# A hybrid state-space and attention inference step: ScalarE's function tables loaded by a dummy activation ahead of its waits

## The chip, the cores and the metric

One core of a Trainium2 chip runs the whole program in one launch. The metric is the device time of one execution in microseconds (us), lower is better; a kernel's time is the median of its runs. The profile is of one execution, and its times count from the start of its span.

## The reference

Two trunk layers over 384 tokens (128 prompt tokens, 256 latent ones) of width 1024, all in float32. Each layer is a mixer and then a mixture of experts, each behind an RMS norm with a shift, a scale and a gate from the conditioning.

```
def trunk_layer(x, mod, g_mix, g_ffn, mixer, p, moe_p, pos, ctx):
    sh1, sc1, gt1, sh2, sc2, gt2 = jnp.split(mod, 6, axis=-1)
    h = rms_norm(x, g_mix) * (1 + sc1) + sh1
    out, state = mixer(h, p, pos, ctx)
    x = x + gt1 * out
    h = rms_norm(x, g_ffn) * (1 + sc2) + sh2
    x = x + gt2 * moe_ffn(h, *moe_p)
```

Layer 0's mixer runs 16 state-space heads in both directions (chunks of 128 tokens, with `decay = exp(...)` of running sums, and `y = rms_norm(y * silu(z), g)` at the end) beside 8 latent attention heads (q and k RMS-normed, softmax). Layer 1's mixer is grouped-query attention with 16 query heads. The experts are 16, of which each token uses 2; their gate is `silu`, the router a sigmoid.

ScalarE is asked for four kinds of function here: Exp (decays, softmax, router), Sqrt (every RMS norm), Silu (conditioning, convolution, z, experts) and Ln (softplus). Copy, Identity and Square run whatever table is loaded.

## The kernel before

The program is written by engine: each engine has one list of instructions, and semaphores order them. TensorE (PE) does matmuls and transposes into PSUM; VectorE (DVE) and ScalarE (ACT) empty the PSUM banks. PE's results go round through five banks in a list of `jobs` of fixed order; each job names the engine that empties it. `take(name)` in ScalarE's list waits until PE has filled the job's bank (`job_done`); `emptied_by` or a `sem_inc` on `free_act` gives the bank back. PE's `fill(name)` waits until the bank of five jobs before has been given back.

The weights come through a ring of eight 1.5 MB slots, loaded by SyncE's queue in the order of use.

The stages, in order of time:

- The first six slots of the modulation weights (`ada(0)` to `ada(5)`). For each, PE multiplies a row of 384 (L467), ScalarE copies it out (`copy_row`, L1144), and PE turns it by three small matmuls (`turn_row`, L479). With row 3, ScalarE squares x (L982), and before row 4 it takes the root (`root_of(0, 0)`, through `root` at L969).
- Layer 0's input projection, the convolution and its Silu.
- The state-space scan: four steps in `STEPS`, of which the last three are full (`i` = 1, 2, 3). A full step has eight "segments": PE spreads a sum, DVE adds the mask (L1722), ScalarE takes Exp (L1226), GpSimd adds two of them (L1908), DVE multiplies (L1732), PE multiplies by x (L834). It ends in a **tail**: DVE forms the gated output (L1748 to L1752, `ysq_ready`), ScalarE squares it and sums the squares (L1234), takes the root of the sum (`ynorm_ready`), DVE inverts it and scales the output (L1754, L1755, `ynormed`), PE transposes it (L863, job `yT`), ScalarE copies it out with a gain (L1241). The other 26 modulation rows are spread over the scan and the preparation of attention (the table `LATE`); two of them lie in each tail, one before the square and one behind the root, and one after the tail.
- The preparation of layer 0's attention: seven blocks of queries and keys, each with a root of its sums (`qk_root`), a normalisation on DVE and transposes (L894) that ScalarE copies out (L1272). The last modulation row is copied in the last turn, between root and copies; PE turns it and drains at once (`late_ada("mla", k)`), and goes on to the transposes behind it.
- Layer 0's attention (`attention("mla", ...)`): 24 units. PE computes scores (L518), DVE their maximum (L1454, `max_ready`), ScalarE Exp with its sum (L1027), PE transposes (L525) and multiplies by the values (L549). The scores of the sixth unit need the bank that ScalarE's first Exp empties.
- The output projection with the residual on DVE, then `moe(0)`: squares, root and router, then the experts.
- Between the layers the three token tiles come one after another: PE mixes a tile's expert rows (L747), DVE adds it to x (L1625), ScalarE squares it (L1000), PE sums (L496), ScalarE takes the root (L969), DVE inverts it (L1380) and scales (L1386), ScalarE shifts (L1013). DVE's list has the first tile's inverse (`normaliser_of_tile(0)`) ahead of the third tile's addition, whose two halves each wait for PE's mixing of that tile.
- Layer 1: input projection (L918) tile by tile with roots, transposes (L906) copied out at L1291, attention with 48 units, output projection, `moe(1)`.

No table load stands in the kernel's text. The build puts an `ACT_TABLE_LOAD` in front of an activation whose function isn't in the loaded table, and the load carries the line of that activation. The helper that gives the last wait its name `link` waits for ScalarE's own instruction just before:

```
            def link(ins):
                n_chain[0] += 1
                ins.then_inc(S["chain_act"], 1)
                act.wait_ge(S["chain_act"], n_chain[0])
```

`moe` already has two dummy activations of one column, `A(table, ones[:, 0:1], ACT.Sqrt)` and the same with Exp (L1062, L1066); `table` is a spare column of `misc` that nobody reads.

Of the kernel before, what the change touches and what calls it, by code (L numbers as in the profile page):

```python
# [26 lines left out]
NT = T // P  # L27
# [49 lines left out]
def build(nc, small_d, x_d, w_d, y_d, stf_d, stb_d, ckv_d, kpe_d, gk_d, gv_d):  # L77
    f32 = mybir.dt.float32
    ALU = mybir.AluOpType
    ACT = mybir.ActivationFunctionType  # L80
# [4 lines left out]
    with ctx:  # L85
# [18 lines left out]
        ident, ones = sm("ident"), sm("ones")  # L104
# [138 lines left out]
        N_PREP = NT + 4  # L243
# [699 lines left out]
        def _(act):  # L943
# [20 lines left out]

            A = act.activation

            def root(out, src, n, scale=1.0):

                return A(out, src, ACT.Sqrt, bias=EPS / (scale * scale), scale=1.0 / (n * scale * scale))  # L969
# [89 lines left out]

            def moe(l):  # L1060
                act.wait_ge(S["x_new"], DC * l + 1)
                A(table, ones[:, 0:1], ACT.Sqrt)  # L1062
                squares(l, 1)
                act.wait_ge(S["tokens_summed"], l + 1)
                root(rt3[6], ps[:, 6, 0:NT], D).then_inc(S["tokens_root"], 1)
                A(table, ones[:, 0:1], ACT.Exp)  # L1066
                act.wait_ge(S["logits_ready"], l + 1)
                A(rt48[0], rt48[1], ACT.Exp, scale=-1.0).then_inc(S["rt_exp"], 1)
                act.wait_ge(S["inverse_spread"], l + 1)
                act.copy(rn_ffn, ps[:, 7, 0:T]).then_inc(S["inverse_copied"], 1)  # L1070
                for n in ("gk", "gv") if l else ():
                    act.wait_ge(outs[n], 16)
                for c in range(6):
                    scale_and_shift(l, c)
                turned_tokens(l, 0)
                for c in range(6, DC):
                    scale_and_shift(l, c)
                turned_tokens(l, 1)
                over = some_beyond(act, l)
                n0 = N_BLOCK * l  # L1080

                def turned_rows(i):
                    if i >= N_BLOCK:
                        return
                    act.wait_ge(S["turned0"], n0 + i + 1)
                    act.copy(xgT[:, i % NR, 0:512], ps[:, 3, :]).then_inc(S["xgT_act"], 1)

                def silu(i):
                    act.wait_ge(S["up_done"], n0 + i + 1)
                    A(sil_of[i % NR], ps[:, i % NR, 0:256], ACT.Silu).then_inc(S["sil_ready"], 1)  # L1090

                def turned_act(i):
                    act.wait_ge(S["act_turned"], n0 + i + 1)
                    act.copy(actT_of[i % NR], ps[:, i % NR, 0:256]).then_inc(S["actT_ready"], 1)

                def rows_out(i):
                    act.wait_ge(S["down0"], n0 + i + 1)
                    if n0 + i >= 2:
                        act.wait_ge(y_stored[i % 2], 16 * ((n0 + i) // 2))
                    act.copy(ysb[i % 2][:, 0:512], ps[:, 6, :]).then_inc(S["y_act"], 1)  # L1100

                def store(i):
                    act.wait_ge(S["y_act"], n0 + i + 1)
                    act.wait_ge(S["y_dve"], n0 + i + 1)
                    act.dma_start(block_of(rows_d, i), ysb[i % 2]).then_inc(y_stored[i % 2], 16)

                for r in range(NR):
                    turned_rows(r)
                for g in range(NG):
                    i = NR * g  # L1110
                    silu(i)
                    silu(i + 1)
                    turned_rows(i + 3)
                    silu(i + 2)
                    turned_rows(i + 4)
                    turned_act(i)
                    turned_act(i + 1)
                    turned_rows(i + 5)
                    rows_out(i)
                    turned_act(i + 2)  # L1120
                    store(i)
                    rows_out(i + 1)
                    store(i + 1)
                    rows_out(i + 2)
                    store(i + 2)

                with act.If(over):
                    B = BEYOND[l]
                    with act.Fori(0, NE) as e:
                        for b in range(N_BEYOND):  # L1130
                            act.wait_ge(B["turned"], e * N_BEYOND + (b + 1))
                            act.copy(xgb[1][:, 0:512], ps[:, 3, :]).then_inc(B["xgT"], 1)
                            act.wait_ge(B["up"], e * N_BEYOND + (b + 1))
                            A(sil_of[0], ps[:, 0, 0:256], ACT.Silu).then_inc(B["sil"], 1)
                            act.wait_ge(B["act_turned"], e * N_BEYOND + (b + 1))
                            act.copy(actT_of[0], ps[:, 5, 0:256]).then_inc(B["actT"], 1)
                            act.wait_ge(B["down"], e * N_BEYOND + (b + 1))
                            act.copy(ysb[0][:, 0:512], ps[:, 6, :]).then_inc(B["y"], 1)
# [11 lines left out]
            for n in range(N_FIRST):  # L1150
                if n == N_SQUARE:
                    squares(0, 0)
                if n == N_SQUARE + 1:
                    root_of(0, 0)
                copy_row(n)
# [50 lines left out]
            for i, (t, full) in enumerate(STEPS):  # L1206
                if i:
                    act.wait_ge(S["xtok_used"], i)
                for k in range(2):
                    b = take("xt", i, k)  # L1210
                    emptied_by(act.copy(xtok[:, 512 * k:512 * k + 512], b[:, :]))
                b = take("bt", i)
                emptied_by(act.copy(Btok, b[:, 0:P]))
                act.wait_ge(S["free_act"], emptied[index[("bt", i)]][1])
                act.sem_inc(S["xtok_ready"], 1)
                if i == 0:
                    late_rows("state")
                if full:
                    for g in range(2):
                        b = take("g", i, g)  # L1220
                        emptied_by(act.copy(Gs2[g], b[:, 0:P]))
                    act.wait_ge(S["free_act"], emptied[index[("g", i, 1)]][1])
                    act.sem_inc(S["g_ready"], 1)
                    for u in range(8):
                        act.wait_ge(S["seg_ready"], 8 * nfull + u + 1)
                        A(dec[u % 6], dec[u % 6], ACT.Exp).then_inc(S["dec_ready"], 1)  # L1226
                        if u % 2:
                            late_rows("unit", i, {1: -1, 5: 0, 7: 1}.get(u))
                    late_rows("unit", i, 2)
                    late_rows("unit", i, 3)  # L1230
                    for n in LATE[("tail", i)][:1]:
                        copy_row(n)
                    act.wait_ge(S["ysq_ready"], nfull + 1)
                    link(A(zs3[:, t, :], ytok, ACT.Square, accum_out=ssd_r))  # L1234
                    root(ssd_r, ssd_r, D).then_inc(S["ynorm_ready"], 1)
                    for n in LATE[("tail", i)][1:]:
                        copy_row(n)
                    for k in range(2):
                        b = take("yT", i, k)
                        for c in range(4):  # L1240
                            ins = A(oTy3[:, 4 * k + c, TILE[t]], b[:, P * c:P * c + P], ACT.Copy, scale=ssdn[:, 4 * k + c:4 * k + c + 1])  # L1241
                        emptied_by(ins)
                    late_rows("end", i)
                    nfull += 1

            by_head = lambda ap, n: ap.rearrange("p (h n) -> p h n", h=n)
            for k in range(N_PREP + 1):
                v = k - 1
                if k:
                    qk_root(v, mss[v % 2], QM, QM ** -0.5 if v < NT else 1.0)  # L1250
                if k < N_PREP:
                    s, x, sq = k - NT, mkt[k % 2], msq[k % 2]
                    for hh in range(2):
# [21 lines left out]
            attention("mla", HM, m_att, mP)  # L1275
            moe(0)

            squares_of(0)
            squares_of(1)
            root_of_tile(0)  # L1280
# [14 lines left out]
            for i in range(NT + 1):  # L1295
                if i < NT:
# [9 lines left out]
                    A(gsq[t], qkv3[:, t, 0:HQ * HD], ACT.Square).then_inc(S["gsq_ready"], 1)  # L1306
                    qk_root(N_PREP + 2 * i, gss[t], HD, HD ** -0.5)
                    qk_root(N_PREP + 2 * i + 1, gss[NT + t], HD, 1.0)
                if i == 0:
                    shift_of_tile(2)  # L1310
                    turn_gqa(gkT3[:, :, P * KSLOT[3]:P * KSLOT[3] + P], "gkT", 3)
                else:
                    t = ORDER[i - 1]
                    for k in range(2):
                        turn_gqa(gqT3[:, 4 * k:4 * k + 4, TILE[t]], "gqT", t, k)
                    turn_gqa(gkT3[:, :, P * KSLOT[t]:P * KSLOT[t] + P], "gkT", t)
# [705 lines left out]
```

## Time and profile before

| | |
|---|---|
| runs | 1074.12, 1074.91 and 1068.78 us; median 1074.12 |
| the profiled execution | 1069.52 us, span 1068.0 us |
| TensorE (PE) busy | 911.9 us, 85% of the span |
| VectorE (DVE) busy | 338.7 us, 32% |
| ScalarE (ACT) busy | 274.6 us, 26%, 660 instructions |
| mean granted TensorE clock | 0.92 of full speed |
| bytes moved by DMA | 259.00 MB, mean 243 GB/s |

Busy times don't add up to the span, since the engines run beside each other. Outside the span the profiled execution has 1.52 us. "Idle" in square brackets is the time for which an engine stood still just before an instruction, with the engine and line that ended it.

### The profile page before, as it was taken

How to read it: one execution, taken by the hardware profiler on the slowest of the kernel's cores; microseconds unless marked ns; L12 is line 12 of the kernel's file. 1: busy time of each engine (PE TensorE's matmuls, PEld its weight loads, DVE VectorE, ACT ScalarE, POOL GpSimd, SP SyncE). 2: the span in 40 equal slices, each digit the busy share in tenths (PEclk: the TensorE clock that was granted, in tenths of full speed). 3: DMA queues.
4: the chain of work that ended last, by engine and by line, in shares of the span. 5: the costliest groups of instructions: out<-in, count | busy, mean ns of one | idle time of the engine just before them, and what ended most of it. 6: DMA issues, size and time to landing. Idle time of an engine off the chain costs nothing.

```text
span 1068.0 us, 14085 instructions
## 1 busy us (share of the span) xinstructions
PE 911.9 (85%) x5747; PEld 495.2 (46%) x5747; DVE 338.7 (32%) x825; ACT 274.6 (26%) x660; POOL 85.1 (8%) x96
## 2 busy tenths in 40 slices
PE   4999988686888889957989986997999957989984
PEld 1555645464644555533332326654655533333324
DVE  0422005645538630040110113374562140110112
ACT  2411023232336520051210112223552041210210
POOL 2400000110100001050000002000000150000002
PEclk8999998977879999967999997999899967999997
DMA  9999999953367302135899977115000335899925
GB/s 383 427 425 386 369 371 412 384 179 118 128 253 288 123 2 108 70 138 217 355 425 423 423 325 289 66 44 203 1 1 2 118 146 209 352 427 404 422 102 186
DMA packets 36339, 259.00 MB, mean 243 GB/s; under 512 B 3408, under 2 KB 3552, under 8 KB 21424
## 3 DMA queue, kind: packets, MB, share of 16 engines
q1 hardware_dynamic: 20448, 198.27, 46.2%
q0 software_dynamic: 12224, 47.01, 11.9%
q10 hardware_dynamic: 3600, 12.78, 3.0%
q8 instruction: 48, 0.79, 0.3%
q14 instruction: 19, 0.16, 0.0%
HBM read 236.73 MB, written 54.87 MB: 273 GB/s over the span
## 4 chain that ended last, share of the span: by engine, by line
PE 72%; DVE 9%; DMA 8%; ACT 6%; issue 3%; POOL 1%; SPq 0%; PEld 0%; DVEq 0%; POOLq 0%; PEldq 0%; ACTq 0%
PE ps L504 21%; PE ps L671 14%; PE ps L693 8%; PE ps L918 6%; DMA U<-expert_rows 3%; PE ps L518 3%; PE ps L655 3%; PE ps L467 2%; DMA ring<-w_in 2%; PE ps L525 2%; PE ps L747 2%; PE ps L549 1%; ACT hT L1052 1%; DMA expert_rows<-U 1%; PE ps L479 1%
## 5 line engine op out<-in xcount | busy, mean ns | idle before, releaser
L671 PE MATMUL ps<-ring,U 128*32 128x512 f32 x1200 | 166.4, 593 | 0.0
L504 PE MATMUL ps<-U,ring 128*128 128x384 f32 x320 | 106.4, 489 | 3.8 <-DVE U L1470 2.5
L671 PEld LDWEIGHTS ps<-ring,U 128*32 128x32 f32 x1200 | 47.2, 110 | 86.0 <-issue 86.0
L693 PE MATMUL ps<-ring,U 128*32 128x512 f32 x672 | 85.7, 594 | 0.0
L504 PEld LDWEIGHTS ps<-U,ring 128*128 128x128 f32 x320 | 59.6, 189 | 48.0 <-issue 5.0
L671 PE MATMUL ps<-hT,U 128*32 128x512 f32 x168 | 73.1, 592 | 0.0
L671 PE MATMUL ps<-U 128*32 128x512 f32 x168 | 73.1, 592 | 0.0
L467 PE MATMUL ps<-ring,cond_w 128*32 128x384 f32 x512 | 58.6, 583 | 15.4 <-ACT cond_w L974 8.5
L655 PE MATMUL ps<-small,U 128*128 128x128 f32 x192 | 32.6, 326 | 39.3 <-DMA U<-expert_rows 37.3
L918 PE MATMUL ps<-ring,hT 128*128 128x384 f32 x192 | 63.2, 488 | 1.5 <-issue 0.8
L504 PE MATMUL ps<-hT,ring 128*128 128x384 f32 x192 | 63.3, 488 | 0.9 <-issue 0.8
L1579 DVE TENSOR_TENSOR U<-ps,U 128x256 f32<-128x256 f32 x24 | 10.1, 422 | 135.2 <-ACT U L1090 135.2
L504 PEld LDWEIGHTS ps<-hT,ring 128*128 128x128 f32 x192 | 36.1, 190 | 27.5 <-issue 3.3
L918 PEld LDWEIGHTS ps<-ring,hT 128*128 128x128 f32 x192 | 36.0, 190 | 27.3 <-issue 3.4
L655 PEld LDWEIGHTS ps<-small,U 128*128 128x128 f32 x192 | 25.4, 165 | 49.7 <-DMA U<-expert_rows 44.6
L518 PE MATMUL ps<-U,hT 64*128 64x128 f32 (+3 forms) x144 | 42.6, 472 | 5.7 <-ACT U L1027 4.0
L747 PE MATMUL ps<-U 128*128 128x128 f32 x192 | 26.4, 307 | 23.4 <-DMA U<-expert_rows,U 23.4
L1587 DVE COPY U<-ps 128x512 f32<-128x512 f32 x24 | 16.6, 692 | 91.3 <-PE ps L693 56.4
L1090 ACT ACTIVATE U<-ps 128x256 f32<-128x256 f32 x24 | 9.2, 385 | 132.0 <-PE ps L671 132.0
L1413 DVE SCALAR_TENSOR_TENSOR xT<-ps,misc,xT 128x128 f32<-128x128 f32 (+1 forms) x32 | 11.9, 412 | 97.6 <-PE ps L504 97.6
L504 PE MATMUL ps<-ring,hT 128*128 128x384 f32 (+1 forms) x144 | 42.0, 451 | 0.5 <-issue 0.5
L1027 ACT ACTIVATE U<-ps,U 128x384 f32<-128x384 f32 (+1 forms) x72 | 36.3, 510 | 21.3 <-PE ps L525 12.8
(298 smaller groups left out, 1285.0 us busy)
## 6 DMA issues: line engine op xcount, KB each, us to landing
ring<-w_in SPq DMA_DIRECT2D x102, 1536.0 KB, 11.1
expert_rows<-w_in POOLq DMA_DIRECT2D x16, 2048.0 KB, 89.5
U<-expert_rows SPq DMA_DIRECT2D x24, 512.0 KB, 6.4
expert_rows<-U ACTq DMA_DIRECT2D x24, 512.0 KB, 9.2
hT<-w_in SPq DMA_DIRECT2D x6, 1536.0 KB, 12.8
U<-w_in SPq DMA_DIRECT2D x6, 1536.0 KB, 16.1
small<-small_in SPq DMA_DIRECT2D x1, 3147.5 KB, 37.3
xT<-x_in SPq DMA_DIRECT2D x1, 1536.0 KB, 16.7
```

The costliest lines, as they stand in the source:

```text
L467: ins = mm(ps[q:q + 32, bank_row, 0:384], cond3[:, k, :], w[:, k, :], start=(k < 4), stop=(k >= 4))
L504: ins = mm(out, lhs(k), rhs(k), start=(k == 0), stop=(k == n - 1))
L518: filled(mm(b[:, 0:nk], q_of(t, h), k_of(h, k0, nk), start=True, stop=True))
L525: ins = pe.transpose(b[:, P * k:P * k + P], Pb[v % N_P][:, P * k:P * k + P], ident)
L655: ins = pe.transpose(ps[:, 3 + h, P * c:P * c + P], xgb[i % NR][:, 512 * h + P * c:512 * h + P * c + P], ident)
L671: ins = mm(ps[q:q + 32, r, :], xgT[:, r, P * k + q:P * k + q + 32], w[e][:, c:c + 512], start=(k == 0), stop=(k == DC - 1))
L693: ins = mm(ps[q:q + 32, 6 + h, :], actT_of[i % NR][:, P * j + q:P * j + q + 32], w[e][:, c:c + 512], start=(j == 0), stop=(j == 1))
L747: ins = mm(ps[:, MIX_BANK[t] + h, P * c:P * c + P], picked[t][q][:, 512 * h + P * c:512 * h + P * c + P], gate_diag[q][t], start=(q == 0), ...
L918: ins = mm(b[:, 0:384], hT[:, k, TILE[t]], w[:, k, :], start=(k == 0), stop=(k == DC - 1))
L1027: A(Pb[u % N_P][:, 0:nk], b[:, 0:nk], ACT.Exp, bias=nm[:, u:u + 1], accum_out=rs[:, u:u + 1]).then_inc(S["e_ready"], 1)
L1413: ins = stt(xT[:, c, SEG[s]], b[:, SEG[s]], gt[:, 2 * c + s:2 * c + s + 1], xT[:, c, SEG[s]], MUL, ADD)
L1587: dve.tensor_copy(ysb[i % 2][:, 512:1024], ps[:, 7, :]).then_inc(S["y_dve"], 1)
```

## The change

A helper `load_table(function)` issues the dummy activation. It replaces the two dummies in `moe` with the same thing, and is called at these new places:

1. at the start, with Sqrt, behind the squares and ahead of `copy_row(3)` and the first root;
2. in each of the three tails, with Sqrt, behind the tail's first modulation row and ahead of the wait for `ysq_ready`;
3. in the first two tails, with Exp, behind the root and ahead of the tail's second modulation row;
4. in the last turn of the preparation of layer 0's attention, with Exp, behind the last root and ahead of the last modulation row and two copies;
5. between the layers, with Sqrt, ahead of the squares of the first tile;
6. in layer 1's projection, with Exp, behind the last two roots.

```diff
+            def load_table(function):
+
+                A(table, ones[:, 0:1], function)
...
             for n in range(N_FIRST):
                 if n == N_SQUARE:
                     squares(0, 0)
+                    load_table(ACT.Sqrt)
                 if n == N_SQUARE + 1:
                     root_of(0, 0)
                 copy_row(n)
...
                     for n in LATE[("tail", i)][:1]:
                         copy_row(n)
+                    load_table(ACT.Sqrt)
                     act.wait_ge(S["ysq_ready"], nfull + 1)
                     link(A(zs3[:, t, :], ytok, ACT.Square, accum_out=ssd_r))
                     root(ssd_r, ssd_r, D).then_inc(S["ynorm_ready"], 1)
+                    if i + 1 < len(STEPS):
+                        load_table(ACT.Exp)
                     for n in LATE[("tail", i)][1:]:
                         copy_row(n)
...
                 if k:
                     qk_root(v, mss[v % 2], QM, QM ** -0.5 if v < NT else 1.0)
+                if k == N_PREP:
+                    load_table(ACT.Exp)
                 if k < N_PREP:
...
             attention("mla", HM, m_att, mP)
             moe(0)
 
+            load_table(ACT.Sqrt)
             squares_of(0)
             squares_of(1)
             root_of_tile(0)
...
                     qk_root(N_PREP + 2 * i, gss[t], HD, HD ** -0.5)
                     qk_root(N_PREP + 2 * i + 1, gss[NT + t], HD, 1.0)
+                    if i == NT - 1:
+                        load_table(ACT.Exp)
```

## Rows read from the trace of the kernel before

**Rows 1.** The page's chain of work that ended last, by engine.

```profile
PE 72%; DVE 9%; DMA 8%; ACT 6%; issue 3%; POOL 1%; SPq 0%; PEld 0%; DVEq 0%; POOLq 0%; PEldq 0%; ACTq 0%
```

**Rows 2.** Timeline of ScalarE: start, duration, instruction, idle before it; start, `moe(0)`.

```profile
26.26 1.28 ACT L969 ACT_TABLE_LOAD   x1
28.09 0.49 ACT L969 ACTIVATE U<-ps 128x384 f32<-128x384 f32 x1 [0.55 <-PE ps L490]
...
397.97 0.20 ACT L1062 ACTIVATE misc<-small 128x1 f32<-128x1 f32 x1 [12.21 <-DVE xT L1413]
```

**Rows 3.** Timeline of all engines, first tail and the segments behind it.

```profile
211.45 1.06 ACT L1234 ACTIVATE U<-U 128x1024 f32<-128x1024 f32 x1 [5.34 <-DVE U L1752]
...
212.61 1.28 ACT L969 ACT_TABLE_LOAD   x1
...
214.01 0.46 ACT L1144 COPY U<-ps 128x384 f32<-128x384 f32 x1
...
215.15 1.97 PE L863 MATMUL ps<-small,U 128*128 128x128 f32 x8 [6.67 <-DVE U L1755]
...
230.32 2.40 DVE L1722 SCALAR_TENSOR_TENSOR hT<-ps,U,small 128x128 f32<-128x128 f32 x8 [0.37 <-PE ps L827]
...
231.60 0.63 ACT L1226 ACTIVATE hT<-hT 128x512 f32<-128x512 f32 x1
```

**Rows 4.** Timeline, second tail: PE ahead of and behind its wait.

```profile
254.90 1.50 PE L467 MATMUL ps<-ring,cond_w 128*32 128x384 f32 x16
...
261.03 1.41 PE L863 MATMUL ps<-small,U 128*128 128x128 f32 x8 [4.63 <-DVE U L1755]
...
263.44 2.79 PE L467 MATMUL ps<-ring,cond_w 128*32 128x384 f32 x16
```

**Rows 5.** Windows: us, busy time of each engine, PE's granted clock, DMA.

```profile
215.00:223.00 8.00, 7.17 (x36) 4.90 (x36) 1.32 (x2) 2.65 (x9) 0.00 (x0) 0.50 0.52 183
...
261.00:270.00 9.00, 8.97 (x53) 6.38 (x54) 0.00 (x0) 4.86 (x15) 0.00 (x0) 0.62 0.63 241
```

**Rows 6.** Timeline, third tail.

```profile
291.98 1.06 ACT L1234 ACTIVATE U<-U 128x1024 f32<-128x1024 f32 x1
...
294.88 0.76 DVE L1755 TENSOR_SCALAR U<-U,misc 128x1024 f32<-128x1024 f32 x1
...
296.29 1.97 PE L863 MATMUL ps<-small,U 128*128 128x128 f32 x8
```

**Rows 7.** Timeline, end of the preparation and start of layer 0's attention.

```profile
350.01 0.21 ACT L969 ACTIVATE U<-U 128x8 f32<-128x8 f32 x1
...
351.16 0.48 ACT L1144 COPY U<-ps 128x384 f32<-128x384 f32 x1 [0.94 <-PE ps L467]
...
352.76 1.05 PE L894 MATMUL ps<-small,U 128*96 128x128 f32 x8 [0.23 <-DVEq L1785]
...
355.76 1.28 ACT L1027 ACT_TABLE_LOAD   x1 [1.08 <-DVE U L1454]
...
357.57 0.91 PE L518 MATMUL ps<-U,hT 96*128 96x384 f32 x2 [0.18 <-ACT U L1027]
```

**Rows 8.** Timeline, last roots of layer 1 and start of its attention.

```profile
737.22 0.20 ACT L969 ACTIVATE U<-U 128x4 f32<-128x4 f32 x1 [0.57 <-DVE U L1433]
...
741.13 0.59 ACT L1291 COPY hT<-ps 128x512 f32<-128x512 f32 x1 [1.83 <-PE ps L906]
...
744.44 1.28 ACT L1027 ACT_TABLE_LOAD   x1 [0.95 <-DVE U L1454]
...
746.24 1.55 PE L518 MATMUL ps<-U,hT 64*128 64x384 f32 x2 [0.92 <-ACT U L1027]
```

**Rows 9.** Timeline between the layers.

```profile
660.68 1.28 ACT L969 ACT_TABLE_LOAD   x1
...
663.27 2.16 DVE L1625 SCALAR_TENSOR_TENSOR xT<-ps,misc,xT 128x128 f32<-128x128 f32 x8
663.49 1.87 PEld L496 LDWEIGHTS ps<-hT,small 128*128 128x128 f32 x16
```

More of the change, by code:

```diff
@@ L1061, in moe @@
                 act.wait_ge(S["x_new"], DC * l + 1)
-                A(table, ones[:, 0:1], ACT.Sqrt)
+                load_table(ACT.Sqrt)
                 squares(l, 1)
@@ L1065, in moe @@
                 root(rt3[6], ps[:, 6, 0:NT], D).then_inc(S["tokens_root"], 1)
-                A(table, ones[:, 0:1], ACT.Exp)
+                load_table(ACT.Exp)
                 act.wait_ge(S["logits_ready"], l + 1)
@@ L1276, in _ @@
             moe(0)
+            load_table(ACT.Sqrt)
             squares_of(0)
@@ L1308, in _ @@
                     qk_root(N_PREP + 2 * i + 1, gss[NT + t], HD, 1.0)
+                    if i == NT - 1:
+                        load_table(ACT.Exp)
                 if i == 0:
```

## The prediction

> **What bounds the kernel now.** I read the page's chain first: TensorE holds 72% of it, ScalarE only 6% [rows 1]. A change on ScalarE can gain only at those few places where TensorE or VectorE stands still for it, and a table load counts there with its own 1.28 us at most. So the question is not how many loads there are but, for each place, who is idle while the load runs, and what comes next if it doesn't. For that I went through the timeline of each place named in the change. The loads are as many after as before: each new dummy takes a load away from the activation behind it. What is added are nine dummies of about 0.20 us each [rows 2].
>
> Two things about the loads are read before any edit is priced. First, a load is already ahead of a wait where the activation has only one: at the start it runs at 26.26 to 27.54, and the root stands 0.55 us more for TensorE; in the expert layer the dummy starts at 397.97 after 12.21 us of idle time, which begins at 385.76 where its load had ended [rows 2]. Second, where the activation waits for two semaphores, as the first Exp of both attentions does, the load itself stands behind one of them (VectorE's maximum, [rows 7, 8]). So part of the change may find nothing left to hide.
>
> A load's price is 1.28 us plus 0.02 us of gaps: in the first tail it begins at 212.61 and the next instruction of ScalarE but one at 214.01, with a root of 0.20 between [rows 3]. The Trainium skill (ScalarE: Activation LUTs, What ACT_TABLE_LOAD costs) gives 1283 ns for the load and some 1380 ns of drain with it, 2.66 us for every switch. The trace agrees on the first number and shows no room for the second. By the page's number each place that gains would gain up to twice as much, 4 us more in all, and the time would be about 1066 us; that is still within one per cent of the median.
>
> **The change part by part.** Negative is faster.
>
> Start (edit 1): nothing. The load is hidden, and TensorE sets the root's start by 0.55 us [rows 2]. At its new place ScalarE stands idle too, before row 3.
>
> First tail (edits 2, 3): this load is on the path. The square starts when VectorE is done, after 5.34 us of idle time; the load, the root, VectorE's inverse and scaling follow one another, and TensorE has been idle for 6.67 us when it starts its transposes at 215.15 [rows 3]. With the load inside the 5.34 us, the root follows the square directly. It must then wait for the square's own result, which the load had hidden. No row shows this wait alone. Below it is nothing; above, the longest gap of a handover in the rows is the 0.23 us of [rows 7]; the square's handover to the load is 0.02. I take 0.05 us, since the wait is on the engine's own result and no drain lies in it, so the gain is 1.30 - 0.05 = 1.25 us, at least 1.05. Behind the root now stand the Exp load and its dummy, 1.28 + 0.20 = 1.48 us, ahead of the modulation row's copy (214.01 before). The root moves from 213.91 to about 212.65, and the copy to 212.65 + 0.10 + 1.48 = 214.2 or 214.3, ended by 214.75. TensorE wants this row when the eight transposes are through, at 215.15 - 1.25 + 1.6 = 215.5 or later, and the first bank of transposes is full at about 215.05. Both come later than the copy, by 0.3 us in the tighter case. The slot of the ring which that copy frees is released 0.2 us later; the next weights are several slots ahead. Cost: nothing.
>
> What the Exp load gives back at its old place, ahead of the next step's first Exp, is nothing either: it ran at 230.30, and that Exp begins at 231.60, while VectorE began the segments at 230.32 with eight in 2.40 us, so the four that this Exp reads were there at 231.52 [rows 3]. The step behind the second tail has the same order of things.
>
> Second tail: the same, -1.25. TensorE is idle 4.63 us before its transposes [rows 4].
>
> Third tail: nothing, perhaps a little tighter. ScalarE doesn't wait before this square (291.98, just behind a copy), so the load is only moved from behind the square to ahead of it, and the dummy is new: the scaling on VectorE would begin at about 294.88 + 0.24 = 295.12 and end at 295.88. TensorE comes out of its modulation row and starts the transposes at 296.29 [rows 6]: 0.4 us of cover is left of 0.65.
>
> Layer 0's attention (edit 4): about nothing, with a gain and a cost of equal size. The gain: the load begins at 355.76 behind the maximum, the first Exp at 357.06 [rows 7]. With the table there, the first Exp starts at 355.78. But TensorE was busy with the first five score blocks until 357.39, and waited only 0.18 us for the sixth. What follows is limited by ScalarE's six Exps in a row; with the load gone they wait for VectorE's maxima instead, and those of a full score block take about as long as the Exps (the sixth is only computed by TensorE from 357.57, 0.18 us earlier at best). Followed block by block, the sixth Exp comes 0.5 us earlier, not 1.3. The cost: the load and dummy now stand at 350.24 to 351.73, and the last modulation row, copied at 351.16 so far, is copied from 351.63: 0.47 later. TensorE waits for it, turns it and drains, and went on to its transposes at 352.76 with 0.23 us of idle time put down to VectorE. If the drain is what took these 0.23 us, the transposes come 0.45 later; if it was VectorE, 0.25. I take 0.45. Net -0.05, between -0.6 and +0.4.
>
> Layer 1's attention (edit 6): -0.9. Load at 744.44, first Exp at 745.73, and here TensorE has been idle for 0.92 us when it gets the bank at 746.24 [rows 8]. That is all it can gain: it finished the five blocks at 745.32. TensorE runs slowly here, 1.55 us for this block and the transposes behind it, so VectorE's maxima are ready before it and all of the 0.92 should come through; the bounds are 0 and 0.92. The load's new place is after the root at 737.22. Three copies stand behind it and move from 737.33 to about 738.85, and end at about 740.8; the next copy waits for TensorE until 741.13, so 0.3 us of cover is left. VectorE needs only the roots, which are ahead of the load.
>
> Between the layers (edit 5): -0.4. The load is on the chain: it starts at 660.68, the root follows, VectorE inverts and adds the third tile from 663.27 [rows 9]. Without it VectorE would be ready 1.28 us sooner, at 661.99. But the second half of that tile is late next: TensorE's mixing goes on until it begins the following sums at 663.5 or 663.6 [rows 9], and VectorE gets it some 0.2 us later, at 663.8. Four of the eight additions are then left, 1.1 us, and the scaling starts at 664.93 instead of 665.35. Gain 0.42; the bounds are 0 and 1.28.
>
> Sum: -1.25 - 1.25 - 0.05 - 0.9 - 0.4 = -3.85 us, or 0.4%. The profiled execution of 1069.52 us (1068.0 of span and 1.52 around it) would become 1065.7 us. That execution was near the fast end of the runs shown, 4.6 us under their median of 1074.12. On the median I predict **1070 us**. Nothing later takes it back: the DMA engines are nearly idle before both output projections, and the weights of the experts wait for slots that TensorE frees, so they move with it.
>
> **The rivals.**
>
> *The clock stays up in the second tail.* Today TensorE's granted clock falls to half after the idle time there: a modulation row takes 1.50 us before it and 2.79 behind [rows 4], and the clock over 261 to 270 is 0.62 [rows 5]. TensorE's idle time falls from 4.63 to 3.4 us. If that keeps it at 2.4 GHz, the row gives 1.29 us and the transposes and small turns around it, which are as much work again, about as much: -2.6 on top, some 1067 us. Against it: in the first tail the idle time stays at 5.4 us, and there the clock is 0.50 behind it [rows 5].
>
> *The clock falls in one place more.* This is the case on the slow side. Every wait of TensorE moves by one or two microseconds against the points at which the clock changes. A further stretch like 215 to 223, where TensorE was busy for 7.17 us at 0.50 [rows 5], does work in it that the full clock does in 3.6, so it costs 3.6 us. It decides from 3.9 us on, so a bit more than one such stretch must be added; with one and a half it is +1.5 us, about 1076 us. The place is the scan, where low and full stretches alternate. For it: nothing holds the clock in place, and the runs shown differ by 6 us with the same program. Against it: the change shortens TensorE's waits there.
>
> *The change doesn't do what it says.* If the load in the tails is not on the path after all, or the root's wait for the square costs as much as the load did, or the cover of 0.3 us in the tails (a copy behind the Exp load) is gone, the two tails give nothing or lose 0.2 each. Then attention and the seam leave -1.3: 1073 us. For it: the loads at the start and in the expert layers are ahead of their waits already [rows 2].
>
> **How the numbers follow.** The forecast as summed has 0.55, the clock that stays up 0.18, the clock that falls once more 0.12, the change without effect 0.12, and 0.03 is left for a load that costs up to twice its row. That last one is the Trainium skill's price for a switch. Around each case lies the spread of the runs, about 3 us to each side. A measurement of this kernel can't tell less than one per cent, 10.7 us. Faster than 1063.4 us is only reached from the fast end of the first rival: 0.07. Slower than 1084.9 would need several low stretches more: 0.03. The range goes from 1067 with 4 off for the spread, 1063, to the slow case at 1076 and half a microsecond more, 1076.5.
>
> **What the profile after would show.** In the first two tails: a load between the copy of row one and the square, root at once behind the square (under 0.15 us), transposes 1.25 us after where they would be, an Exp load behind the root, and no load at the first Exp of the next step, which still starts when VectorE lets it. TensorE's idle time before L863 falls from 6.67 and 4.63 to 5.4 and 3.4. Third tail: transposes directly behind TensorE's own row. Layer 0's attention: TensorE's turn of the last modulation row waits 0.5 us more, the sixth block no longer for ScalarE. Layer 1: the 0.92 us gone. Between the layers VectorE's additions split in two fours with a gap. I would be wrong if ScalarE's root stood long behind the square without a load, if the copies behind the Exp loads became what TensorE waits for, or if the granted clock in 200 to 310 changed by more than these microseconds.

## The result and the profile after

The changed kernel takes 1067.57 us (median of 20 runs), the kernel before 1074.27 (20 runs): ratio 0.9946, 95% interval 0.9930 to 0.9962. That is 5.8 us faster, between 4.1 and 7.5. I had forecast 1070, from a sum of -3.85. One run of a kernel below, others_again, took 1167.52 us at a clock of 0.795: it is in a slower state of the chip, and only the median of its row has it.

The profiled execution is one of the longest of its kernel: 1073.41 us, at a mean granted clock of 0.912, where the 20 runs have 0.918. So its span can't be set against that of before. Its pieces can, each from its own start. From the page: the span, the busy times, the granted clock in 40 slices, and the chain.

```profile
span 1071.8 us, 14094 instructions
...
PE 919.4 (86%) x5747; PEld 500.3 (47%) x5747; DVE 338.5 (32%) x825; ACT 276.7 (26%) x669; POOL 85.0 (8%) x96
...
PEclk8899997688879899977999998998899967999997
...
PE 72%; DVE 8%; DMA 8%; ACT 5%; issue 3%; POOL 1%; PEld 1%; SPq 0%; DVEq 0%; POOLq 0%; PEldq 0%; ACTq 0%
```

Nine instructions more on ScalarE, which are the nine dummies; its share of the chain is 5% for 6. The windows show where this execution lost its time. First before, then after; the columns are those of [rows 5], the clock is the third figure from the end:

```profile
170.00:205.00 35.00, 29.34 (x257) 20.48 (x255) 23.78 (x49) 10.15 (x21) 5.09 (x4) 1.00 1.02 425
```

```profile
170.00:205.00 35.00, 28.18 (x188) 19.89 (x189) 20.87 (x45) 9.03 (x19) 5.08 (x4) 0.79 1.01 405
```

In the same 35 us TensorE ran 257 matmuls before and 188 after. This stretch lies ahead of the first tail, and the two kernels have the same instructions in it, in the same order. At its start the execution after is 0.8 us early; by the first square it is 9.9 us late (221.39 for 211.45); by its last instruction only 3.8. Nor is that the work of the edits: the executions of others_only and others_again, one and the same kernel, have that square at 222.78 and 216.39. So a gain of 3 to 6 us can't be read off one pair of profiles.

The first tail, in order of time:

```profile
220.13 1.23 DVE L1765 TENSOR_TENSOR U<-U 128x1024 f32<-128x1024 f32 x1
221.39 1.06 ACT L1240 ACTIVATE U<-U 128x1024 f32<-128x1024 f32 x1 [2.31 <-DVE U L1765]
222.35 0.19 ACT L1240 ACTIVATION_READ_ACCUMULATOR U<-U 128x1 f32 x1
222.57 0.20 ACT L973 ACTIVATE misc<-misc 128x1 f32<-128x1 f32 x1
222.79 1.28 ACT L969 ACT_TABLE_LOAD   x1
...
223.81 1.28 PE L863 MATMUL ps<-small,U 128*128 128x128 f32 x8 [3.88 <-DVE U L1768]
224.08 0.20 ACT L969 ACTIVATE misc<-small 128x1 f32<-128x1 f32 x1
224.19 0.46 ACT L1148 COPY U<-ps 128x384 f32<-128x384 f32 x1
224.55 2.18 ACT L1249 ACTIVATE U<-ps,small 128x128 f32<-128x128 f32 x8
```

The root stands 0.03 us behind the square's sum (222.54), with no load between, and TensorE's transposes start 2.42 us after the square where it was 3.70 [rows 3]: -1.28. The Exp load runs while VectorE and TensorE go on. The second tail has the same 2.42.

The same timeline at the start of layer 0's attention, at the seam between the layers, and at the start of layer 1's attention; first the rows of before that the last two are measured from:

```profile
659.60 1.06 ACT L1000 ACTIVATE hT<-xT 128x1024 f32<-128x1024 f32 x1 [2.52 <-DVE xT L1625]
...
665.35 2.18 DVE L1386 SCALAR_TENSOR_TENSOR hT<-xT,misc,U 128x128 f32<-128x128 f32 x8
...
743.54 1.78 PE L518 MATMUL ps<-U,hT 64*128 64x128 f32 x10 [0.67 <-ACT U L1291]
...
747.73 0.69 PE L525 MATMUL ps<-small,U 128*128 128x128 f32 x2
```

```profile
353.75 0.21 ACT L973 ACTIVATE U<-U 128x8 f32<-128x8 f32 x1
353.98 1.28 ACT L969 ACT_TABLE_LOAD   x1
...
355.38 0.46 ACT L1148 COPY U<-ps 128x384 f32<-128x384 f32 x1
...
355.90 0.83 PE L479 MATMUL ps<-misc,U 128*128 128x2 f32 x6 [1.15 <-ACT U L1148]
356.96 1.23 PE L894 MATMUL ps<-small,U 128*96 128x128 f32 x8 [0.23 <-issue]
...
664.92 1.06 ACT L1004 ACTIVATE hT<-xT 128x1024 f32<-128x1024 f32 x1 [2.51 <-DVE xT L1638]
...
665.88 0.26 ACT L973 ACTIVATE U<-ps 128x128 f32<-128x128 f32 x1
...
667.40 1.12 DVE L1638 SCALAR_TENSOR_TENSOR xT<-ps,misc,xT 128x128 f32<-128x128 f32 x4 [0.28 <-PE ps L747]
...
669.12 1.13 DVE L1638 SCALAR_TENSOR_TENSOR xT<-ps,misc,xT 128x128 f32<-128x128 f32 x4 [0.59 <-PE ps L747]
670.16 2.18 DVE L1399 SCALAR_TENSOR_TENSOR hT<-xT,misc,U 128x128 f32<-128x128 f32 x8
...
748.37 3.38 PE L518 MATMUL ps<-U,hT 64*128 64x128 f32 x12 [0.68 <-ACT U L1302]
...
749.59 0.37 ACT L1031 ACTIVATE U<-ps,U 128x128 f32<-128x128 f32 x1 [1.27 <-DVE U L1467]
...
751.67 0.72 PE L525 MATMUL ps<-small,U 128*128 128x128 f32 x2
```

Layer 0: from the last root to TensorE's transposes 3.21 us where it was 2.75 [rows 7], +0.46. The 0.23 us ahead of them are still there, now put down to nobody, although VectorE was done earlier against them; what is left in the program at that place is the drain. Layer 1: TensorE's score blocks run on as one group of 12 where the gap of 0.92 us was [rows 8], and from the first scores to the first transposes it is 3.30 us for 4.19, -0.89. These two don't have the same clock: over the first 1.78 us of the scores it was 1.00 in the execution before and 0.50 in that after. At half clock throughout, the three executions without edit 6 (tails_only, mla_only, before_warm) take 4.58 or 4.59 us and seven with it 3.30 to 3.32. So at equal clock the edit takes off 1.28 us, the whole load, and not the 0.92 of the gap. Seam: VectorE's eight additions have become two fours, each waiting for TensorE, as the second half's lateness demanded; from the second tile's square (659.60 before) to the first scaling 5.24 us for 5.75, -0.51.

The start (edit 1) moved nothing that shows: the root waits for TensorE's sum with the load ahead of it or not, and comes at about 28 us where that sum ran at full clock and at 29.4 to 30 where it ran at half clock. Both are seen in kernels with the edit and without it.

The pieces add up to -2 x 1.28 - 0.9 - 0.5 + 0.46 = -3.5 us, or -3.9 with the 1.28 of equal clock in layer 1's attention. The measured gain is 5.8. The experiments ask first whether each piece is what it seems, and then where the other 1.9 to 2.3 us come from.

### The profile page after: what moved, and what is told of

Read it like the earlier page. It is cut to its first block, busy times and chain, and to the rows that moved or that the text cites. A ratio compares the mean times of both kernels' runs of the same rounds, so it can differ in the third digit from the quotient of the medians.

```text
span 1071.8 us, 14094 instructions
## 1 busy us (share of the span) xinstructions
PE 919.4 (86%) x5747; PEld 500.3 (47%) x5747; DVE 338.5 (32%) x825; ACT 276.7 (26%) x669; POOL 85.0 (8%) x96
## 4 chain that ended last, share of the span: by engine, by line
PE 72%; DVE 8%; DMA 8%; ACT 5%; issue 3%; POOL 1%; PEld 1%; SPq 0%; DVEq 0%; POOLq 0%; PEldq 0%; ACTq 0%
PE ps L504 21%; PE ps L671 13%; PE ps L693 8%; PE ps L918 6%; PE ps L518 3%; DMA U<-expert_rows 3%; PE ps L655 3%; PE ps L467 3%; PE ps L747 2%; PE ps L525 2%; DMA ring<-w_in 2%; PE ps L549 1%; ACT hT L1056 1%; DMA expert_rows<-U 1%; PE ps L827 1%
## 5 line engine op out<-in xcount | busy, mean ns | idle before, releaser
L518 PE MATMUL ps<-U,hT 64*128 64x128 f32 (+3 forms) x144 | 46.1, 512 | 4.2 <-ACT U L1031 2.7
```

What stands on the lines that cost most here:

```text
L518: filled(mm(b[:, 0:nk], q_of(t, h), k_of(h, k0, nk), start=True, stop=True))
```

## The experiments

Each kernel was timed in five rounds beside the kernel before. The granted clock has two levels, 1.2 and 2.4 GHz, so 2 x (1 - mean clock) x span is the time that an execution spent at 1.2 GHz. "Low" is its mean over a kernel's runs; its standard error is about 2 us, or 3 with the kernels of six runs (tail_slow, warm_tails, warm_two_tails; the others have 12, after 20). The row of before is from all 87 of its runs in these rounds. That of after is from its own 20, which were timed in other rounds, so its low time is set against before's only across sessions.

| kernel | edits | median us | ratio (95%) | mean clock | low us |
|---|---|---|---|---|---|
| before | | 1073.4 to 1075.3 | 1 | 0.9138 | 184.8 |
| after | 1 to 6 | 1067.57 | 0.9946 (0.9930 to 0.9962) | 0.9179 | 175.2 |
| tails_only | 2, 3 | 1068.91 | 0.9960 (0.9936 to 0.9983) | 0.9153 | 181.0 |
| sqrt_tails | 2 | 1071.12 | 0.9962 (0.9946 to 0.9979) | 0.9135 | 185.0 |
| others_only | 1, 4, 5, 6 | 1074.46 | 0.9997 (0.9975 to 1.0020) | 0.9139 | 184.5 |
| others_again | 1, 4, 5, 6 | 1073.95 | 0.9990 (0.9972 to 1.0008) | 0.9146 | 182.9 |
| mla_only | 4 | 1072.63 | 1.0005 (0.9984 to 1.0027) | 0.9128 | 186.8 |
| layers_att1 | 5, 6 | 1070.26 | 0.9960 (0.9939 to 0.9981) | 0.9186 | 174.0 |
| tails_layers_att1 | 2, 3, 5, 6 | 1066.40 | 0.9937 (0.9916 to 0.9958) | 0.9193 | 172.0 |
| mla_behind_row | 1 to 6, 4 moved | 1067.38 | 0.9942 (0.9919 to 0.9965) | 0.9187 | 173.2 |
| tail_slow | 1 to 6, two switches more | 1081.34 | 1.0088 (1.0053 to 1.0122) | 0.9098 | 194.9 |
| before_warm | none, idle matmuls | 1073.24 | 0.9989 (0.9961 to 1.0016) | 0.9198 | 171.7 |
| warm_tails | as mla_behind_row, idle matmuls | 1067.00 | 0.9912 (0.9886 to 0.9939) | 0.9225 | 165.1 |
| warm_two_tails | the same, fewer | 1063.79 | 0.9924 (0.9899 to 0.9948) | 0.9210 | 167.9 |

### The tails

The kernel is the changed one with the dummies outside the tails taken out.

> Edits 2 and 3 alone (both loads in the tails), the rest as before. My theory (the loads in the first two tails stood on the path): from the square's start to TensorE's transposes 2.42 us where it was 3.70, in both tails; time 2.5 us under before. Rival 'the clock gives the rest': the measured gain of 5.8 us came mostly from the scan's clock, so this kernel alone gains 4 to 5 us. Rival 'no effect': within 0.5 us of before.

Ratio 0.9960, 4.3 us, and 2.42 us in both tails. The spans are as the theory has them, and the time is nearer to the rival's 4 to 5; the interval (1.8 to 6.9 us) holds both.

The third tail is instructive, since the clock decided there. In the executions of before and after, the modulation row ahead of the transposes ran at half clock (2.79 us), and TensorE came last [rows 6]: 4.68 us from the copy to the transposes before, 4.69 after. In this one it ran at full clock, so ScalarE's chain came last:

```profile
296.59 0.48 ACT L1148 COPY U<-ps 128x384 f32<-128x384 f32 x1 [8.13 <-PE ps L467]
297.09 1.28 ACT L969 ACT_TABLE_LOAD   x1
297.95 1.50 PE L467 MATMUL ps<-ring,cond_w 128*32 128x384 f32 x16
298.50 1.04 ACT L1239 ACTIVATE U<-U 128x1024 f32<-128x1024 f32 x1
...
300.91 1.09 PE L863 MATMUL ps<-small,U 128*128 128x128 f32 x8 [1.46 <-DVE U L1762]
```

From the copy to the transposes it is 4.32 us. The kernel without the tails' edits has the same clock there, and 4.08 (from 301.40 to 305.48):

```profile
301.40 0.48 ACT L1148 COPY U<-ps 128x384 f32<-128x384 f32 x1 [8.12 <-PE ps L467]
301.77 1.06 ACT L1239 ACTIVATE U<-U 128x1024 f32<-128x1024 f32 x1
...
302.94 1.28 ACT L973 ACT_TABLE_LOAD   x1
...
305.48 1.09 PE L863 MATMUL ps<-small,U 128*128 128x128 f32 x8 [1.23 <-DVE U L1765]
```

So a load that is moved where ScalarE doesn't wait gains nothing and costs the dummy, 0.24 us, whenever the cover of a slow TensorE is gone.

Edit 2 without edit 3:

```diff
                     root(ssd_r, ssd_r, D).then_inc(S["ynorm_ready"], 1)
-                    if i + 1 < len(STEPS):
-                        load_table(ACT.Exp)
```

> Edit 2 alone: the Sqrt load ahead of the square in the three tails; the Exp load stays at the first Exp of the next step. My theory (the Exp load costs and gives nothing in either place): the same as with edits 2 and 3, 1069.5 us, tails 2.42 us each, and the first Exp of the next step begins 1.3 us after VectorE began the segments, as in before. Rival: the Exp load on the old place now is late, since the tail ends earlier, and costs up to 1.3 us twice.

Ratio 0.9962 beside 0.9960, tails at 2.42. The rival (up to 2.6 us lost) would have given 0.9984, but the difference of the two kernels has an error of 3 us, so the times alone don't exclude it. The rows behind the first tail do:

```profile
234.48 1.28 ACT L1230 ACT_TABLE_LOAD   x1
235.41 1.13 DVE L1727 SCALAR_TENSOR_TENSOR hT<-ps,U,small 128x128 f32<-128x128 f32 x4 [1.28 <-PE ps L827]
236.57 0.63 ACT L1230 ACTIVATE hT<-hT 128x512 f32<-128x512 f32 x1 [0.81 <-DVE hT L1727]
```

The load is over at 235.76, and the Exp stands 0.81 us more for VectorE. It begins 1.16 us after VectorE's segments, and so it does in tails_only, where the load was moved. At its old place this load was hidden, so edit 3 gains nothing.

### A switch more in each tail

```diff
                     link(A(zs3[:, t, :], ytok, ACT.Square, accum_out=ssd_r))
+                    A(misc[:, 244:245], ones[:, 0:1], ACT.Exp)
+                    A(misc[:, 245:246], ones[:, 0:1], ACT.Sqrt)
                     root(ssd_r, ssd_r, D).then_inc(S["ynorm_ready"], 1)
```

> The changed kernel with two more dummies, Exp and Sqrt, between the square and the root of every tail: two more switches there, each 1.28 + 0.20 us by the trace. If a switch costs what its row shows and the tails are on the path, the first two tails take 3.0 us more each and the third 2.6 (0.4 us of cover): 8.6 us over the changed kernel. If a switch costs 2.66 us, as the Trainium skill has it (ScalarE: Activation LUTs, What ACT_TABLE_LOAD costs), it is 14 to 16 us. If the tails are hidden, under 2 us.

1.0088 over 0.9946 is 1.0143, so 15.3 us over the changed kernel, 11 to 19. Going by the time alone, the 2.66 us that the Trainium skill gives for a switch (ScalarE: Activation LUTs, What ACT_TABLE_LOAD costs) look confirmed. The timeline of the first tail says otherwise:

```profile
215.01 0.19 ACT L1240 ACTIVATION_READ_ACCUMULATOR U<-U 128x1 f32 x1
215.21 1.28 ACT L1241 ACT_TABLE_LOAD   x1
216.50 0.20 ACT L1241 ACTIVATE misc<-small 128x1 f32<-128x1 f32 x1
216.71 1.28 ACT L1242 ACT_TABLE_LOAD   x1
218.01 0.20 ACT L1242 ACTIVATE misc<-small 128x1 f32<-128x1 f32 x1
218.12 0.18 ACT L973 ACTIVATE misc<-misc 128x1 f32<-128x1 f32 x1
...
219.34 1.97 PE L863 MATMUL ps<-small,U 128*128 128x128 f32 x8 [8.26 <-DVE U L1770]
```

5.30 us from the square to the transposes for 2.42: two switches with their dummies cost 2.88, and there is no room for a drain of 1.38 us after either. Three tails make 8.6 us, or 8.3 if the third (5.29 us) is set against the 2.79 of the changed kernel's execution, which had some cover. The low time rose with it, from 175.2 to 194.9 us, while TensorE stands 8.26 us ahead of the first tail's transposes.

What a microsecond at low clock is worth can be read off without any edit: over the 87 runs of the kernel before, a line through time against low time has a slope of 0.29 us per us. So 19.7 us more are 5.7, and 8.6 + 5.7 = 14.3 us, beside a difference of means of 13.9. The slope is a correlation in one kernel and not an experiment, and the twelve other kernels, 6 to 20 runs each, have slopes from 0.21 to 0.52; that it fits here is the check that it gets. The low time and the time also come from the same runs, so a fit says that the excess came with the clock and not what moved the clock.

### Does TensorE's idle time bring the clock down?

If so, work without use in the idle time brings it up. Five matmuls go ahead of TensorE's wait, into the bank that the transposes overwrite:

```diff
-                    pe.wait_ge(S["ynormed"], nfull + 1)
+                    yT = [fill("yT", i, 0)]
+                    for _ in range(5):
+                        mm(yT[0][:, 0:T], ident, small[:, OFF["tri_f"][0]:OFF["tri_f"][0] + T], start=True, stop=True)
+                    pe.wait_ge(S["ynormed"], nfull + 1)
...
-                        b = fill("yT", i, k)
+                        b = yT[0] if k == 0 else fill("yT", i, 1)
```

> The kernel before with the same five idle matmuls in each tail and no load moved. Theory A: its low-clock time, 184 us, falls to 170 or less and the time by 3 to 5 us, to about 1069, without any dummy. Theory B: 1073 as before.

> The kernel of the run before with the load behind the row, and in each tail five matmuls of 128x384 by TensorE ahead of its wait for the normalised output, into the bank that the transposes overwrite; they compute nothing that is used (1.6 us at full clock, inside an idle time of 3.7 to 5 us). Theory A (TensorE's idle time in the tails is what brings its clock down, so that a microsecond of idle costs more than itself): the low-clock time per run, twice one minus the mean clock times the span, falls from 173 us to 160 or less, and the time by 3 us or more, to 1064. Theory B (the low stretches come as they come): both unchanged within 2 us.

The clock followed in both: low time 184.8 to 171.7 us with the kernel before, 173.2 to 165.1 on the changed one. For the first, the difference is about six standard errors, and theory B is out; for the second it is two, which alone would show little. The time of the first did not follow as I had said: 0.9989 (1.2 us under before, between 4.2 under and 1.7 over). The second has 0.9912 beside 0.9942, 3.2 us less with an error of 3.8. The matmuls were dearer than reckoned, 0.70 us each for my 0.33 (3.49 us for five at full clock), and stood on the path: 3.98 us from square to transposes in the second tail of both, for 3.70 and 2.42, and in the third 9.07 with the kernel before and 6.26 on the changed one, for 4.31 there and 2.41 in the kernel without them. With the kernel before that is 0.3 + 4.8 = 5.0 us of added path; by the slope, 13.1 us less at low clock give back some 3.8 of it, an estimate.

With `range([5, 2, 0][nfull])`:

> As the kernel with five idle matmuls in each tail, but five in the first tail, two in the second and none in the third: they took 0.7 us each, not the 0.33 that I had reckoned, and stood on the path in the second and third tail (3.98 and 6.26 us from the square to the transposes where 2.42 is the least). Theory A: the low-clock time stays at 165 to 170 us, the tails are at 2.42 again, and the time is 3 to 4 us under the same kernel without them, 1063. Theory B (the clock's gain was the work itself): 1067.

2.42 again in the first two tails, 2.50 in the third, low time 167.9 (for 173.2, within the error of 4), and 1063.79 us, ratio 0.9924. This is the fastest median of all, 3.8 us under the changed kernel or 2.4 by the ratios, but the ratios' intervals (0.9899 to 0.9948 and 0.9930 to 0.9962) overlap, and against the same kernel without the matmuls (0.9942) the gain of 1.9 us is within its error of 3.6. That idle matmuls raise the clock is shown on the kernel before; that they pay is not.

```profile
257.91 1.56 PE L861 MATMUL ps<-small 128*128 128x384 f32 x4
...
261.45 1.09 PE L866 MATMUL ps<-small,U 128*128 128x128 f32 x8 [1.99 <-DVE U L1771]
```

L861 is the idle work of the second tail (each matmul has two records), L866 the transposes, now with 1.99 us of idle time for the 4.63 of [rows 4] and the 3.31 of the same kernel without them.

### The places outside of the tails

> Edits 1, 4, 5 and 6 alone; both tails as before. My theory: 1.4 us under before (0.9 at layer 1's attention, 0.5 between the layers, nothing at layer 0's). Rival: 3 to 4 us under, if what I missed lies outside of the tails. From the second tile's square to the first scaling 5.24 us as in the changed kernel (5.75 before).

Ratio 0.9997: 0.3 us, where my sum was -1.4; the interval allows 2.7 at most, so the -1.4 is inside it. The spans were all as expected (5.24 at the seam; 3.30 from scores to transposes in layer 1, for 4.19), and with the 0.46 lost in front of layer 0's attention they make -0.9, or -1.3 at equal clock. I took the edits apart.

> Edits 5 and 6 alone (between the layers, layer 1's attention), without that in front of layer 0's attention. Theory: 0.5 and 0.9 us, so 1.4 us under before, 1071.9; the profile has 5.24 us from the second tile's square to the first scaling and 3.3 us from layer 1's first scores to its first transposes, and layer 0's attention as before (2.75 us from the last root to the transposes). If the clock takes it back, as it seems in the run of edits 1, 4, 5 and 6 (1073.1), the spans are shorter and the time is not.

> Edit 4 alone: the Exp load ahead of the last modulation row's copy. Theory by spans: last root to TensorE's transposes 3.21 us (2.75 before), 0.5 of it given back at the first Exps; time as before. Rival: the later transposes bring the clock down and cost 3 us or more.

> Edits 1, 4, 5 and 6 once more, word for word the kernel run before, to have it beside edit 4 alone on the same chip: 1.4 us under before if its first result (0.3 under) was within its error, none if edits 1 and 4 undo the others.

> Edits 2, 3, 5 and 6, without that of the start and that in front of layer 0's attention. If those two edits bring the clock down (the run of edits 1, 4, 5 and 6 gained 0.3 us, that of 5 and 6 alone 4.3), this one is 3 to 4 us under the changed kernel: 1064. If they don't, it is as the changed kernel plus 0.5: 1067 to 1068.

Edits 5 and 6 alone gain 4.3 us (2.0 to 6.6) at a low time of 174.0. That is 2.5 to 2.9 more than their spans give. In this execution the first scores to transposes of layer 1 take 2.27 us, where I had expected 3.3: TensorE's clock was 1.00 over all of it. With edits 1 and 4 beside them, 0.3 and 1.1 us, at 184.5 and 182.9: on average 0.7 with an error of 1.5, beside 0.9 to 1.3 by the spans. Edit 4 alone: 0.5 us slower, -1.7 to +2.9, its transposes at 3.20 for 2.75. In layer 0's attention nothing is given back for that: with edit 4 and without it TensorE runs the first scores at half clock, in whole or in part, in 13 of the 14 profiled executions, and without the load the first Exp then waits for VectorE. From the first scores to the first transposes it is 4.81 us in tails_only, which has the load there, and 4.82 in the kernel of the next section, which has not. Only the execution before had the full clock there, and 3.58. Over the two measurements the pair 1 and 4 takes away some 3.6 us with an error of about 2.7; but on top of the tails it takes 1 us, and within its error nothing (0.9937 beside 0.9946). That edit 4 costs its 0.46 us in the span is shown. Whether it or edit 1 costs more by way of the clock, or whether the 4.3 of edits 5 and 6 was partly chance, stays open.

### The load behind the row

```diff
-                if k == N_PREP:
-                    load_table(ACT.Exp)
                 if k < N_PREP:
...
                 late_rows("mla", k)
+                if k == N_PREP:
+                    load_table(ACT.Exp)
```

> The changed kernel, with the Exp load of layer 0's attention moved from ahead of the last modulation row's copy to behind it, where ScalarE waits 1.77 us for TensorE's transposes. Theory: TensorE's transposes start 2.75 us after the last root as in before (3.21 in the changed kernel) and the first Exp still finds its table: 0.45 us under the changed kernel, which the time can't tell from nothing and the profile can. Rival: the load only moves the delay to the copies behind it, 3.2 us again.

```profile
352.81 0.21 ACT L973 ACTIVATE U<-U 128x8 f32<-128x8 f32 x1
...
353.96 0.48 ACT L1148 COPY U<-ps 128x384 f32<-128x384 f32 x1 [0.94 <-PE ps L467]
...
354.45 1.28 ACT L969 ACT_TABLE_LOAD   x1
...
355.55 1.05 PE L894 MATMUL ps<-small,U 128*96 128x128 f32 x8 [0.23 <-DVEq L1798]
355.75 0.20 ACT L969 ACTIVATE misc<-small 128x1 f32<-128x1 f32 x1
```

2.74 us from root to transposes: the load behind the copy costs nothing there, and the 0.46 is back. In the time (0.9942) it can't be told, as expected.

## Why the prediction was right, and where it was short

The forecast was faster by 3.85 us; measured are 5.8, 4.1 to 7.5. The time, 1067.57, is within the range.

- **Price of a load.** 1.28 us and no drain: right, by the row in every place and by the doubled switch (2.88 for two with dummies).
- **Tails one and two.** -1.25 each said, -1.28 found. The root's wait for the square, bounded by 0.23 and taken at 0.05, is 0.03. TensorE's idle time ahead of the transposes, said to fall to 5.4 and 3.4 us, was 3.88 and 3.66 in the profiled execution, whose clock was another, and 5.39 and 3.26 in that of tails_only. The copy behind the Exp load, said to end at 0.3 us of cover, was nowhere waited for.
- **Third tail.** Right that it gains nothing; the cover that I named (a modulation row at half clock) isn't always there, and then the price is the 0.24 us that I had reckoned for the delay.
- **Seam.** -0.42 said, -0.51 found, with the second half of the mixing as what comes last.
- **Layer 1's attention.** -0.92 said, -0.89 found between the two profiles, but that agreement is luck: their clocks differ there, and at equal half clock it is -1.28. I had taken the gap of 0.92 us ahead of one score block for all that the edit can gain; that holds for the clock of that execution alone. Why it is the whole load at half clock was not followed further.
- **Layer 0's attention.** The cost was right (0.45 said, 0.46 found); the gain of 0.5 was not seen.
- **Exp at its old place.** Worth nothing, right: 0.81 us of waiting are left behind the load.
- **Start.** Worth nothing, right in the rows.

What was short is a term that wasn't in the sum. I had put the clock among the rivals, as an event in the second tail with 0.18 for it and 0.12 against, and at nought in the forecast. The mean clock went from 0.9138 to 0.9179, and low time fell by 9.6 us, across sessions. At 0.29 that is 2.8 us, and with the 3.5 to 3.9 of the spans 6.3 to 6.7, beside 5.8 measured. In the profiled execution itself the second tail's clock still fell (the row behind it took 2.79 us again), so the rival as I described it isn't seen; and the clock over 200 to 310 us was 0.79 for 0.78, so the last sign of being wrong isn't either. So the sum of -3.85 is close for the spans (-3.5 to -3.9) and lies just outside of the measured gain's interval (4.1 to 7.5). With the slower tails the clock moved the other way. That what TensorE does in its waits moves the clock is shown, by the idle matmuls and the slower tails; that the extra 1.9 to 2.3 us of this change are such is argued from the slope. Against it stands edit 2 alone, which gained 4.1 us (2.3 to 5.8) at an unchanged mean clock, where its spans give 2.6; and the whole excess is small enough that the error of the measurement, 1.7 us, holds most of it. How it is shared among the edits stays open. The low time hints at edits 5 and 6: against before in the same rounds (183.6, 186.8 and 184.0 us) it fell by 10 to 13 us in mla_behind_row, layers_att1 and tails_layers_att1, and by less than 3 us, or not at all, in tails_only, sqrt_tails and the two runs of edits 1, 4, 5 and 6. No experiment isolates why.

## What to carry to other kernels

Price a moved wait by who stands still for it, from one row to the next, and check it by the same interval after: most intervals here came within 0.1 us while single executions of one kernel differ by 8 to 12. Look at the clock of both intervals first: one here came out right only because they differed. Put a preload where its engine already waits, behind whatever that engine owes to others and not ahead of it. And where TensorE alternates between work and waits, waits that are made longer can cost more than themselves through the clock: here 13.9 us for 8.3 to 8.6 by the rows. That shorter waits give back as much isn't shown. So a total that fits a rule is not yet evidence for it.

## What was unexpected of the hardware

- Doubling a suspected cost of 8.6 us by the rows cost 14 to 15 in the time, with low time up by 19.7 us.
- Fifteen idle matmuls in three places (some 10 us of work) took 13 us of low time off a run and left its time where it was, with 5.0 us of them on the path.
- A load put by the build ahead of an activation with two waits stands behind VectorE's ([rows 7, 8]), and ahead of the only wait of an activation with one ([rows 2], and the load at 234.48 in sqrt_tails).
